# Twenty-two short series of products, on operands already in place, behind the last product of a three-layer transformer kernel

## The reference

```
h = rms_norm(x, pre_g);  p = split_columns(h @ w_in + b_in)
mix = concat(stick-breaking, native sparse, forgetting and latent attention, each times silu(gate))
x = x + rms_norm(mix @ w_out, post_g)
```

```
h2 = rms_norm(x, norm2_g)
x  = x + (silu(h2 @ w_gate) * (h2 @ w_up)) @ w_down        # inner width 5632
```

## Time and profile before

| what | value |
|---|---|
| time, median of 2 runs | 1979.62 us (1979.48 to 1979.77) |
| profiled execution, span from first to last instruction | 1977.6 us |
| TensorE busy with products | 1963.8 us, 99% of the span, 10170 products |
| loads of the standing operand | 1666.5 us, 84% |
| DVE, ACT, POOL busy | 1145.0, 945.6, 80.1 us |
| granted TensorE clock | full in every slice |
| chain that ended last | PE 97%, DVE 1%, ACT 1% |

### The profile page before, as it was taken

The page is one execution under the profiler, slowest core; times in us unless marked ns, Lnnn a source line. Parts: engine busy times, 40 slices in busy tenths (PEclk is TensorE's granted clock), DMA queues, the critical chain, the costliest instruction groups (busy, mean ns, idle before and its releaser), DMA issues.

```text
span 1977.6 us, 27533 instructions
## 1 busy us (share of the span) xinstructions
PE 1963.8 (99%) x10170; PEld 1666.5 (84%) x10170; DVE 1145.0 (58%) x1352; ACT 945.6 (48%) x1256; POOL 80.1 (4%) x125
## 2 busy tenths in 40 slices
PE   9999999999999999999999999999999999999999
PEld 7898988887899998888778788888888888888887
DVE  6584555556666554655757986645454444444443
ACT  6355444444564554444655564544444444443342
POOL 4000000001200000000300100000000000000000
PEclk9999999999999999999999999999999999999999
DMA  8664555665755445666555435666666666656653
GB/s 289 201 221 125 165 163 164 191 197 158 251 178 193 145 145 150 194 197 187 168 171 161 143 133 181 193 191 191 191 188 184 190 191 189 189 180 214 205 203 128
DMA packets 188153, 360.74 MB, mean 182 GB/s; under 512 B 13202, under 2 KB 20417, under 8 KB 187793
## 3 DMA queue, kind: packets, MB, share of 16 engines
q1 hardware_dynamic: 183408, 346.15, 56.3%
q0 software_dynamic: 4640, 13.20, 2.4%
HBM read 357.20 MB, written 2.10 MB: 182 GB/s over the span
## 4 chain that ended last, share of the span: by engine, by line
PE 97%; DVE 1%; ACT 1%; DMA 0%; issue 0%; ACTq 0%; POOL 0%; DVEq 0%; SPq 0%; POOLq 0%
PE psum L627 26%; PE psum L629 25%; PE psum L628 25%; PE psum L635 3%; PE psum L638 3%; PE psum L637 3%; PE psum L1334 1%; PE psum L745 1%; PE psum L1110 1%; PE psum L759 1%; PE psum L734 1%; PE psum L891 0%; PE psum L1591 0%; PE psum L653 0%; PE psum L655 0%; PE psum L654 0%
## 5 line engine op out<-in xcount | busy, mean ns | idle before, releaser
L593 DVE TENSOR_TENSOR wl<-raw,wh 128x1024 fp32r<-128x1024 f32 (+1 forms) x655 | 775.4, 1196 | 663.2 <-ACT wh L585 656.0
L585 ACT ACTIVATE wh<-raw 128x1024 fp32r<-128x1024 f32 (+1 forms) x655 | 671.9, 1036 | 826.7 <-PE psum L629 681.8
L627 PE MATMUL psum<-wh,xh 128*128 128x512 f32 (+2 forms) x1584 | 615.5, 389 | 5.0 <-DVE xl L929 4.1
L629 PE MATMUL psum<-wh,xl 128*128 128x512 f32 (+2 forms) x1584 | 608.8, 384 | 0.0
L628 PE MATMUL psum<-wl,xh 128*128 128x512 f32 (+2 forms) x1584 | 608.6, 384 | 0.0
L627 PEld LDWEIGHTS psum<-wh,xh 128*128 128x128 f32 x1584 | 297.6, 188 | 67.0 <-DVE xl L929 7.1
L629 PEld LDWEIGHTS psum<-wh,xl 128*128 128x128 f32 x1584 | 297.5, 188 | 58.7
L628 PEld LDWEIGHTS psum<-wl,xh 128*128 128x128 f32 x1584 | 297.8, 188 | 56.7
L635 PE MATMUL psum<-xh,wh 128*128 128x256 f32 x512 | 146.1, 285 | 0.0
L638 PE MATMUL psum<-xl,wh 128*128 128x256 f32 x512 | 144.9, 283 | 0.0
L637 PE MATMUL psum<-xh,wl 128*128 128x256 f32 x512 | 144.9, 283 | 0.0
(11 more groups left out here) (422 smaller groups left out, 1600.8 us busy)
## 6 DMA issues: line engine op xcount, KB each, us to landing
raw<-in_w_in_dram SPq DMA_DIRECT2D x263, 512.0 KB, 4.3
raw<-in_w_out_dram SPq DMA_DIRECT2D x96, 512.0 KB, 3.9
raw<-in_w_gate_dram SPq DMA_DIRECT2D x88, 512.0 KB, 3.6
raw<-in_w_up_dram SPq DMA_DIRECT2D x88, 512.0 KB, 3.6
raw<-in_w_down_dram SPq DMA_DIRECT2D x80, 512.0 KB, 3.6
cmp_raw<-in_cmp_w_dram SPq DMA_DIRECT2D x16, 512.0 KB, 4.4
raw<-in_w_small_dram SPq DMA_DIRECT2D x16, 336.0 KB, 3.1
bias<-in_b_in_dram POOLq DMA_DIRECT2D x18, 256.0 KB, 4.1
```

Source lines behind the costliest of these rows:

```text
L585: act.activation(wh[:, n % SPLIT_SLOTS, 0:k, 0:unit.n], buffer[:, 0:k, 0:unit.n], ACT.Copy).then_inc(hi_done, 1)
L593: dve.tensor_tensor(out=wl[:, n % SPLIT_SLOTS, 0:k, 0:unit.n], in0=buffer[:, 0:k, 0:unit.n], in1=wh[:, n % SPLIT_SLOTS, 0:k, 0:unit.n].bit ...
L627: pe.matmul(o, ah_[:, kt, tok], hi_w, start=first, stop=False)
L629: ins = pe.matmul(o, al_[:, kt, tok], hi_w, start=False, stop=last)
```

## The change

Behind the last `pe_stage` TensorE's program gets 22 series of four or five products, 93 in all. Every one opens and closes its own sum (`start=True, stop=True`) and writes into `st`, whose content nothing reads any more. All operands are tiles that already lie in SBUF, in the type float32r: `ah` as `a_cols` (11264 columns), `al` as `l_cols`, slot 0 of `wh` as `w_cols` (1024 columns), `xh` as `x_cols`. No wait and no signal is added, and no other engine's program changes but for line numbers.

```diff
+            def series(n, out_, lhsT, rhs):
+                for i in range(n):
+                    pe.matmul(out_(i), lhsT(i), rhs(i), start=True, stop=True, skip_group_check=True)
+            a_cols, w_cols, x_cols = (t.rearrange("p a b -> p (a b)") for t in (ah[:, :, :], wh[:, 0, :, :], xh[:, :, :]))
+            l_cols = al[:, :, :].rearrange("p a b -> p (a b)")
+            def bank(n, m=P):
+                return lambda i: st[0:m, 0:n]
+            def turn_banks(n):
+                return lambda i: st[:, i % 4 * 512:i % 4 * 512 + n]
+            def apart(i):
+                return st[:, 0:512].rearrange("p (h q) -> p h q", h=2)[:, :, P:T]
+            def piece(t, c0, n):
+                return lambda i: t[:, c0:c0 + n]
+            series(4, bank(512), piece(a_cols, 0, P), piece(w_cols, 0, 512))
+            series(5, turn_banks(512), piece(a_cols, 0, P), piece(w_cols, 0, 512))
+            series(5, bank(256), piece(w_cols, 0, P), piece(x_cols, 0, 256))
+            series(5, apart, piece(w_cols, 0, P), piece(x_cols, 0, 256))
+            series(5, turn_banks(256), piece(w_cols, 0, P), piece(x_cols, 0, 256))
+            series(5, bank(256), lambda i: w_cols[:, i * P:i * P + P], piece(x_cols, 0, 256))
+            series(4, bank(512), piece(w_cols, 0, P), piece(a_cols, 0, 512))
+            series(4, bank(512), piece(a_cols, 0, P), piece(a_cols, 2048, 512))
+            series(4, bank(512), piece(a_cols, 4, P), piece(w_cols, 0, 512))
+            series(4, bank(512), piece(a_cols, 16, P), piece(w_cols, 0, 512))
+            series(4, bank(512), piece(a_cols, 64, P), piece(w_cols, 0, 512))
+            series(4, bank(512), piece(w_cols, 0, P), piece(a_cols, 4, 512))
+            series(4, bank(512), piece(w_cols, 0, P), piece(a_cols, 16, 512))
+            series(4, bank(512), piece(w_cols, 0, P), piece(a_cols, 64, 512))
+            series(4, bank(512), piece(w_cols, 0, P), piece(a_cols, 256, 512))
+            series(4, bank(512, 64), piece(a_cols, 0, 64), piece(w_cols, 0, 512))
+            series(4, bank(512, 96), piece(a_cols, 0, 96), piece(w_cols, 0, 512))
+            series(4, bank(384), piece(a_cols, 0, P), piece(w_cols, 0, 384))
+            series(4, bank(480), piece(a_cols, 0, P), piece(w_cols, 0, 480))
+            series(4, bank(512), piece(a_cols, 0, P),
+                   lambda i: a_cols[:, 2048:3072].rearrange("p (a b) -> p a b", a=2)[:, :, 0:256])
+            series(4, bank(512), piece(l_cols, 0, P), piece(a_cols, 0, 512))
+            series(4, bank(512), piece(x_cols, 0, P), piece(x_cols, 2048, 512))
```

## The result

The change takes 1995.33 us, median of two runs (1994.87 and 1995.79), against 1979.62: a ratio of 1.0077, 95% interval 1.0061 to 1.0093. The forecast was 1994.9, in a range of 1993.5 to 1999.5, less than 2% over the time before. The profiled execution is the longer one, 1995.79 us with a span of 1994.0; the other run's span is 1993.1.

A forecast was written before the change was run, and what follows sets the result against it. TensorE was taken to bound the kernel: 18.7 us of added products, 3.4 us hidden beside the tail, cost 15.3; the span ends at 1992.9, plus 2.0 us around it gives 1994.9 us, range 1993.5 to 1999.5.

The forecast's parts named there:

- What bounds the kernel: Whole span: TensorE, with products in flight for 99% of it, sets the time up to the last few microseconds.
- The price of the products: 93 added products cost their distances between starts: 0.227 us at 512 columns, 0.120 at 256; sum 18.7 us.
- the near end of the odd places: Series 9 to 14 and 20, shifted or cut operands: 0.233 us a product, +0.2 us; the far end was +5.0 us.
- the 36 products said to stand in the trace: Series 1 to 3, 5 to 7, 15, 21: same tiles and bank use claimed already present in the old kernel's trace.
- The cover of the tail: Behind the last old product: 3.4 us of added products lie beside DVE's last addition and the store, costing nothing.
- The start and the end: Added stretch: starts 0.227 us after the last old product, old waits cost nothing; 0.3 us for the engines' final meeting.
- Rival 1: Shifted, cut or shared operands (series 8 to 14, 20, 22) run at half pace: 6.5 us more, 2001.9 with series 4; chance 0.12.
- Rival 2: Added products on the same operands run at their columns' bare pace: about 1.0 us less, 1993.9 us; chance 0.08.
- Rival 3: Each added product waits for the one before: 51.5 us instead of 18.7, time 2027.7 us, +2.4%; chance 0.02.
- Rival 4: Added series are dropped, or the span ends with the output: time stays 1979.6 us; chance 0.01.

The follow-up runs named there:

- run 16: Not a run's label: the words advise series of 16 or more products. Thirteen series of 16 products in place of the 22 series measured 2023.67 us.

## Why the prediction was right

- **What bounds the kernel**: right. Before, the chain ran through TensorE up to the tail, and now TensorE ends it; SP waits for it for 15.6 us.
- **The price of the products**: 18.7 us forecast, 18.9 in the change, 18.7 for the same columns in plain places. The distance of 0.120 holds, and 0.227 where a series is settled; over all 65 products of 512 columns it is 0.2295. The 384- and 480-column products, interpolated at 0.174 and 0.214, follow each other after 0.173 to 0.182 and 0.212 to 0.221 us. The 0.2 us on top were forecast as the near end of the odd places; they lie partly on other series than named there (7, 8 and 21 inherited theirs). One reading was wrong and cost nothing: no row of before moves 512 columns of `ah`, as series 7, 15 and 21 do, so only 24 of the 36 products said to stand in the trace do.
- **The cover of the tail**: 3.4 us forecast; 14 products of 3.2 us cost nothing, and the same series ahead of the tail cost 3.6 us more than behind it.
- **The start and the end**: no gap at the old stage's waits; 0.24 us from the last product to the end of the span, 0.3 forecast. The span was 1994.0 instead of 1992.9, mostly because the old part was 0.97 us longer in that execution. The prediction counts an old part that ends at another time as a sign of being wrong and has no term for it beyond 0.3 us of spread between runs. That spread was too small: 15 runs of the kernel before lie between 1979.25 and 1980.73. Against their median the plain and the reversed series cost 15.1 and 15.3 us, with 15.3 forecast. What lies around the span was 1.7 to 1.9 us in every run that has both numbers, not 2.0; this took back 0.2 us of the longer span, so that the total came a little nearer than its terms.
- **Rival 1** (odd places at half pace): wrong; the worst kept place costs 3%, and series 4, with gaps in its output, runs at 0.120 like its neighbours 3 and 5. The Trainium skill, PSUM — Partial Sum Buffer, section Specifications (TRN2), says that patterns that are not contiguous slow matmuls significantly; this does not show in series 4.
- **Rival 2** (bare pace on the same operands): wrong for float32r; the extra belongs neither to a change of operands nor to adding to a sum, since 65 equal opening products keep it (each still with its own load). Bfloat16, at 0.216, doesn't have it.
- **Rival 3** (each waits for the one before): wrong here. Where it was made true, its price was near for 512 columns (0.558 against 0.58); for the others it had no term for the lower clock.
- **Rival 4** (the series don't run or end nothing): wrong; all 93 stand in the trace, and the end waits for them.

## What to carry to other kernels

Price independent products behind a chain that TensorE bounds by the distance between starts, not by the duration, which is 1.7 times as long here at 512 columns, and take off only what the program's tail hides. In the places tried, where operands lie in SBUF, which bank is written or whether an output has gaps was worth at most 3% in this kernel; a wait between two products of 512 columns was worth 0.33 us at the full clock. Short series of four carry the rhythm of what ran before them: to compare places, run 16 or more, with a plain series between.

## What the runs showed that was not expected

- Float32r products of 512 columns have a steady distance of 0.2267 us and an unsettled one that wanders between 0.224 and 0.236, the same to a nanosecond in two executions of one order. A plain series returns to the steady one in four to six products; a standing operand 64 bytes off its tile's start never did in 16: its distances alternate between 0.236 and 0.231.
- The load of 128 standing columns takes 0.19 us in float32r and 0.10 in bfloat16, and in the run with waits 0.29 at the lower clock.
- The first 48 us of the program vary between executions: the old part ended 0.1 to 1.7 us later than in the trace of the kernel before. The two largest delays, 1.4 and 1.7 us, and the change's come at the same places, the rise of the clock and the wait at 46 to 48 us.
